# Split weights in 24 tiles of the first mixer, and one ScalarE pass a chunk behind six norms

## The reference

```
def hgrn2_mixer(h, w_in, lb, norm_g, w_out):
    proj = h @ w_in
    q, f_fw, f_bw, i_in, g = jnp.split(proj, 5, axis=-1)
    ...
    def gates(f_logit):
        f = lb + (1.0 - lb) * jax.nn.sigmoid(f_logit.astype(jnp.float32))
        return heads(jnp.log(f)), heads(1.0 - f)
    ...
    o = rms_norm(o_fw + o_bw, norm_g.reshape(HG_HEADS, HG_DV)) * jax.nn.silu(g)
    return o.reshape(B, S, D_MODEL) @ w_out
```

## Time and profile before

| | |
|---|---|
| median of three runs | 3061.45 us (3059.26 to 3065.03) |
| profiled execution | 3059.53 us, span 3057.8 us |
| instructions | 57758 |
| TensorE busy | 2936.9 us, 96% of the span |
| VectorE busy | 2234.3 us, 73% |
| ScalarE busy | 1633.3 us, 53% |
| granted TensorE clock, mean | 0.989 of full |
| bytes moved | 503.04 MB, 165 GB/s on average |

### The profile page before, as it was taken

One profiled execution on the slowest core, in us unless ns is written; L12 is line 12 of the kernel. 1 busy time (PEld: TensorE's weight loads), 2 busy tenths in 40 slices (PEclk: granted clock), 3 DMA queues, 4 the chain that ended last, 5 costly groups with the idle time before them and its releaser, 6 DMA issues.

```text
span 3057.8 us, 57758 instructions
## 1 busy us (share of the span) xinstructions
PE 2936.9 (96%) x19592; PEld 2665.4 (87%) x19592; DVE 2234.3 (73%) x4764; ACT 1633.3 (53%) x3372; POOL 62.1 (2%) x112
## 2 busy tenths in 40 slices
PE   7988999999999999999999999999999999998998
PEld 6888899999887778899999988888898889797896
DVE  6346498888779985649888877777585578656686
ACT  2113557778544443655777854444554267463574
POOL 3000000000001100000000000000000000000000
PEclk9999999999999999999999999999999999999999
DMA  9521454444478853445444455555441145432453
GB/s 397 200 76 55 146 187 161 152 164 139 159 258 309 308 200 118 144 155 186 158 153 163 139 172 187 190 186 190 136 138 63 56 164 177 144 132 79 145 174 117
DMA packets 137686, 503.04 MB, mean 165 GB/s; under 512 B 15312, under 2 KB 15440, under 8 KB 137264
## 3 DMA queue, kind: packets, MB, share of 16 engines
q1 hardware_dynamic: 122544, 445.63, 43.1%
q0 software_dynamic: 14976, 55.19, 5.0%
HBM read 498.65 MB, written 2.10 MB: 164 GB/s over the span
## 4 chain that ended last, share of the span: by engine, by line
PE 81%; DVE 5%; ACT 4%; issue 1%; DVEq 0%; ACTq 0%
PE PB L536 14%; PE PB L537 14%; PE PB L538 13%; PE PA L579 9%; PE PA L580 9%; PE PA L578 9%; PE PA L772 4%; PE PB L526 2%; DVE w_low L2223 2%; PE PA L984 1%; PE PA L1157 1%; PE PA L627 1%; ACT h_high L1301 1%; DVE BIG L2249 1%; ACT w_high L1198 1%
## 5 line engine op out<-in xcount | busy, mean ns | idle before, releaser
L1198 ACT ACTIVATE w_high<-ring 128x512 fp32r<-128x512 f32 x1548 | 962.3, 630 | 848.8 <-PE PA L580 466.4
L2223 DVE TENSOR_TENSOR w_low<-ring,w_high 128x512 fp32r<-128x512 f32 x1548 | 1050.7, 690 | 430.3 <-ACT w_high L1198 414.6
L536 PE MATMUL PB<-h_high,w_low 128*128 128x256 f32 x3792 | 1088.4, 287 | 30.4 <-DVE h_low L1889 20.7
L537 PE MATMUL PB<-h_low,w_high 128*128 128x256 f32 x3792 | 1071.8, 283 | 0.0
L538 PE MATMUL PB<-h_high,w_high 128*128 128x256 f32 x3792 | 1069.5, 282 | 0.0
L536 PEld LDWEIGHTS PB<-h_high,w_low 128*128 128x128 f32 x3792 | 725.2, 191 | 46.6 <-issue 25.0
L537 PEld LDWEIGHTS PB<-h_low,w_high 128*128 128x128 f32 x3792 | 719.4, 190 | 0.7 <-issue 0.5
L538 PEld LDWEIGHTS PB<-h_high,w_high 128*128 128x128 f32 x3792 | 718.4, 189 | 0.0
L578 PE MATMUL PA<-w_low,a_high 128*128 128x512 f32 x1200 | 470.3, 392 | 7.9 <-DVE a_low L2232 7.1
L579 PE MATMUL PA<-w_high,a_low 128*128 128x512 f32 x1200 | 476.3, 397 | 0.0
L580 PE MATMUL PA<-w_high,a_high 128*128 128x512 f32 x1200 | 474.0, 395 | 0.0
(11 more groups left out here) (334 smaller groups left out, 2587.3 us busy)
## 6 DMA issues: line engine op xcount, KB each, us to landing
ring<-tiles SPq DMA_DIRECT2D x842, 512.0 KB, 3.3
BIG<-ada POOLq DMA_DIRECT2D x96, 512.0 KB, 7.1
BIG<-skew POOLq DMA_DIRECT2D x4, 512.0 KB, 4.7
X<-x SPq DMA_DIRECT2D x1, 1024.0 KB, 5.8
skew<-BIG POOLq DMA_DIRECT2D x1, 1024.0 KB, 6.4
out<-X SPq DMA_DIRECT2D x4, 256.0 KB, 2.1
con<-consts SPq DMA_DIRECT2D x1, 911.0 KB, 8.8
BIG<-masks POOLq DMA_DIRECT2D x1, 768.0 KB, 8.4
```

What stands on the lines that cost most here:

```text
L536: mm(dst, lhs_l, high, start=start, stop=False, skip_group_check=True)
L537: mm(dst, lhs_h, low, start=False, stop=False, skip_group_check=True)
L1198: fn(tile_half(w_high, s, b), ring[:, at:at + HALF], ACT.Identity).then_inc(sem("high_ready"), 1)
L2223: tt(tile_half(w_low, s, b), ring[:, at:at + HALF], tile_half(w_high, s, b).bitcast(F32), ALU.subtract).then_inc(sem("low_ready"), 1)
```

## The change

The 40 tiles of `hg_in` become two runs: `hg_decays`, 16 whole tiles, and `hg_rest`, 24 split tiles. The activations of that mixer now lie in `HB`, since `w_high` lies over `H`, and are split as well: ScalarE rounds four pairs behind its eight affine passes, VectorE subtracts. The masks of the lower triangle move from the buffer of `w_low` into `TMP`. TensorE's sum over the partitions of vectors 2 to 5 stands behind 11 split tiles; the last of these vectors is accumulated by VectorE block by block between the splits of the first eight tiles, and the decays are made chunk by chunk between the others.

Behind the six norms ScalarE makes one pass a chunk, in place. The rounding of pairs 0 and 1 goes to VectorE (`HIGH_BY_ACT`), as a copy ahead of its subtraction; that of pairs 2 and 3 is one ScalarE pass each over both chunks, behind the in-place passes. Pair 0 is copied and subtracted ahead of VectorE's fourth scaling.

```diff
-    ("hg_in", 5 * DC), ("hg_out", DC), ("wq0", 2 * PEER_HEADS), ("keys0", 2), ("experts0", 2 * NKEYS),
+    ("hg_decays", 2 * DC), ("hg_rest", 3 * DC), ("hg_out", DC), ("wq0", 2 * PEER_HEADS), ("keys0", 2), ("experts0", 2 * NKEYS),
 ...
-        way_masks, w_low = overlaid("way_masks", 2 * TILE, ("w_low", 2 * TILE))
+        w_low = sb("w_low", 2 * TILE, F32R)
 ...
-        LOW_MASKS = way_masks[:, 0:PAIR_LEVELS * P]
+        LOW_MASKS = TMP[:, 0:PAIR_LEVELS * P]
 
         SUMS = ["experts0", "experts1", "down0", "down1"]
+        HIGH_BY_ACT = 2
 ...
-            def split_linear(name, order=(0, 1, 2, 3)):
+            def split_linear(name, order=(0, 1, 2, 3), first=0, last=None):
 
                 s0, (q0, n) = SPLIT_AT[name][0], product_at[name]
-                h0 = fresh_pairs(order)
+                h0 = None if first else fresh_pairs(order)
 
                 def body(k, it):
                     pe.wait_ge(taken, it * 4 + (q0 + k - 3))
                     split_product(product_slot(q0 + k), s0 + k, it, 4, h0 if k == 0 else None)
 
-                spans(pe, body, (0, n))
+                spans(pe, body, (first, n if last is None else last))
 ...
             pe.wait_ge(sem("mod_ready"), w.up(sem("mod_ready"), 2))
-            linear("hg_in", H, sem("h_ready"), 0, 3 * DC)
+            linear("hg_decays", HB, sem("h_ready"))
+            split_linear("hg_rest", last=11)
             ada(2, LATER)
-            linear("hg_in", H, None, 3 * DC)
-            all_taken("hg_in")
+            split_linear("hg_rest", first=11)
+            all_taken("hg_rest")
             pe.wait_ge(sem("mod_ready"), w.up(sem("mod_ready")))
 ...
-            def split_evacuate(run, first):
+            def split_evacuate(run, first, at=0, func=lambda j: ACT.Identity, edge=None):
 ...
+                edges = (2, first + 2, first + 3) if first else (2, 3)
 ...
-                    fn(BIG[:, bass.ds(it * (4 * T) + j * T, T)], product_slot(q0 + j),
-                       ACT.Identity).then_inc(taken, 1)
+                    fn(BIG[:, bass.ds(it * (4 * T) + (at + j * T), T)], product_slot(q0 + j),
+                       func(j)).then_inc(taken, 1)
 ...
-                spans(act, tile, (2, first + 2, first + 3, n) if first else (2, 3, n))
+                spans(act, tile, edges + ((edge + 2, n) if edge else (n,)))
                 copied(n - 2)
                 copied(n - 1)
 ...
@@ -1297,11 +1300,13 @@
                         act.wait_ge(sem("scaled"), w.up(sem("scaled")))
                     dk, g = dst[:, m * T:(m + 1) * T], gain[:, m:m + 1]
                     add = {} if shift is None else {"bias": shift[:, m:m + 1]}
-                    if split:
-                        fn(h_high[:, m * T:(m + 1) * T], dk, ACT.Identity, scale=g, **add)
                     ins = fn(dk, dk, ACT.Identity, scale=g, **add)
                     if m % 2:
                         ins.then_inc(sem(name), 1)
+                        w.up(sem(name))
+                        if split and m // 2 >= HIGH_BY_ACT:
+                            act.wait_ge(sem(name), w.value(sem(name)))
+                            fn(two(h_high, m // 2), two(dst, m // 2), ACT.Identity).then_inc(sem("pair_high"), 1)
 
             def norm_affine(i, split=True):
                 affine(X, p("ln_g", i * DC, DC), p("ln_b", i * DC, DC), "x_out", split)
@@ -1310,6 +1315,11 @@
 
                 if sub:
                     affine(HB, gains(layer, sub), modulation(layer, sub, 0), "whole_ready", split=True)
+                elif layer == 0:
+                    affine(HB, gains(layer, sub), modulation(layer, sub, 0), "h_ready")
+                    for i in range(DC // 2):
+                        act.wait_ge(sem("h_ready"), i + 1)
+                        fn(two(h_high, i), two(HB, i), ACT.Identity).then_inc(sem("pair_high"), 1)
                 else:
                     affine(H, gains(layer, sub), modulation(layer, sub, 0), "h_ready")
 ...
             modulated(0, 0)
-            evacuate("hg_in", big(0, 16 * T), ACT.Sigmoid, 0, 2 * DC)
-            evacuate("hg_in", big(16 * T, 16 * T), ACT.Identity, 2 * DC, 4 * DC)
-            evacuate("hg_in", HG_G, ACT.Silu, 4 * DC, 5 * DC)
+            for k in range(2):
+                evacuate("hg_decays", big(14 * k * T, 16 * T), ACT.Sigmoid, 14 * k, 14 + k)
+                split_high("hg_rest", k)
+            evacuate("hg_decays", big(15 * T, T), ACT.Sigmoid, 15)
+            split_evacuate("hg_rest", 0, 16 * T, lambda j: ACT.Identity if j < 2 * DC else ACT.Silu, 2 * DC)
             act.wait_ge(sem("ada_psum"), 2)
             split_high("hg_out", 0)
             split_high("hg_out", 1)
 ...
-            def scale(dst):
+            def scale(dst, name=None):
 
                 dve.wait_ge(sem("root_ready"), w.up(sem("root_ready")))
                 v.reciprocal(inv[:, :], inv[:, :]).then_inc(sem("dve_step"), 1)
                 dve.wait_ge(sem("dve_step"), w.up(sem("dve_step")))
                 for i in range(DC // 2):
+                    if i == DC // 2 - 1 and name is not None:
+                        split_fresh(dst, name, 0)
                     tt(chunks(two(dst, i)), chunks(two(X, i)), over(inv[:, :], 2), ALU.mult)\
                         .then_inc(sem("scaled"), 1)
+                if name is not None:
+                    for i in range(1, DC // 2):
+                        split_fresh(dst, name, i)
 ...
-            def split_whole(src, name):
-                for i in range(DC // 2):
-                    split_pair(src, name, i)
-
-            def split_x():
-                split_whole(X, "x_out")
-
-            def rms(name, dst, run=None):
+            def split_fresh(src, name, i):
+
+                dve.wait_ge(sem(name), w.up(sem(name)))
+                if i < HIGH_BY_ACT:
+                    v.tensor_copy(two(h_high, i), two(src, i)).then_inc(sem("dve_step"), 1)
+                    dve.wait_ge(sem("dve_step"), w.up(sem("dve_step")))
+                else:
+                    dve.wait_ge(sem("pair_high"), w.up(sem("pair_high")))
+                tt(two(h_low, i), two(src, i), two(h_high, i).bitcast(F32), ALU.subtract)\
+                    .then_inc(sem("h_split"), 1)
+
+            def rms(name, dst, run=None, split=None):
                 if name is not None:
                     dve.wait_ge(*added(name, DC - 1))
                 if run is not None:
                     split_low(run, 0)
                 w.up(sem("squares_ready"), DC // 2)
-                scale(dst)
+                scale(dst, split)
                 if run is not None:
-                    split_whole(dst, "whole_ready")
                     split_low(run, 1)
 ...
-                scale(X)
-                if run is not None:
-                    split_x()
+                scale(X, "x_out" if run is not None else None)
 ...
-            rms(None, H)
+            rms(None, HB)
             for k in range(DIRECT, DC):
                 ada_tile(1, k, 0, first=DIRECT)
             modulate(0, 1, PB, P)
             modulate(1, 2, PB[:, 1024:], P)
-            ada(2, LATER)
-            modulate(2, LATER)
-            for d, way in enumerate(HG["ways"]):
-                dve.wait_ge(taken, (d + 1) * DC)
-                for m in range(DC):
-                    s_ = slice(m * T, (m + 1) * T)
-                    ts(way["f"][:, s_], way["f"][:, s_], om[:, m:m + 1], lb[:, m:m + 1],
+            for i in range(DC // 2):
+                split_pair(HB, "pair_high", i)
+            ada(2, LATER - 1)
+            for k in range(3 * DC):
+                split_low("hg_rest", k)
+                if k < DC:
+                    ada_tile(LATER - 1, k, 0)
+                if k == 12:
+                    modulate(2, LATER)
+                d, m = divmod(k - DC, DC)
+                if d >= 0:
+                    f, s_ = HG["ways"][d]["f"], slice(m * T, (m + 1) * T)
+                    dve.wait_ge(taken, d * DC + m + 1)
+                    ts(f[:, s_], f[:, s_], om[:, m:m + 1], lb[:, m:m + 1],
                        ALU.mult, ALU.add).then_inc(sem("dve_step"), 1)
-                dve.wait_ge(sem("dve_step"), w.up(sem("dve_step"), DC))
+                    w.up(sem("dve_step"))
+            for way in HG["ways"]:
+                dve.wait_ge(sem("dve_step"), w.value(sem("dve_step")))
                 ts(way["k"], way["f"], -1.0, 1.0, ALU.mult, ALU.add).then_inc(sem("dve_step"), 1)
                 w.up(sem("dve_step"))
             dve.wait_ge(sem("dve_step"), w.value(sem("dve_step")))
@@ -2582,11 +2609,11 @@
             dve.wait_ge(sem("way_masks_loaded"), w.up(sem("way_masks_loaded"), 16))
             dve.wait_ge(taken, 3 * DC)
             decay_attention(HG, "hg_out")
-            all_taken("hg_in")
+            all_taken("hg_rest")
             gated_heads(HG_MIX, HG_HEADS, lambda h: p("hg_norm_g", h, 1), HG_G)
             scale_heads(HG_MIX, HG_HEADS)
             add_product("hg_out", modulation(0, 0, 2))
-            rms("hg_out", HB, "wq0")
```

(12 more changed lines are left out.)

2 lines of the change are left out of this document (1 added, 1 removed).

## The result

The changed kernel took 3029.03 us (median of four runs, 3025.99 to 3029.45), the kernel before 3060.36 us beside it (3058.54 to 3065.03): ratio 0.9894, 95% interval 0.9882 to 0.9907, so 1.1% faster. The forecast was 3032.6, with a range of 3024.5 to 3042. The profiled execution took 3028.78 us, its span is 3027.1, 30.7 shorter than before.

The account below looks back on a forecast made before the run. TensorE was taken as the bound, with 81% of the chain. 14.9 us from 24 split tiles plus 13.9 us from six norms made 28.8, giving 3032.6 us against the median of 3061.45; range 3024.5 to 3042.

Parts of the forecast that it names:

- 24 x 0.62 = 14.9: First mixer: each of 24 tiles, once split, falls from 3.45 to 2.83 us, gaining 14.9 us.
- Late transfers at no cost: First mixer: VectorE's later start delays transfers; tiles 16 to 19 still in time, cost 0, range 0 to 5; rival 0.10.
- room for two split tiles: First mixer: each tile may be split while two earlier ones are multiplied, so a late one has about a tile's time.
- my own signs of being wrong: TensorE waiting for w_low between 97 and 125, a modulation block after 115, extra table loads after tile 32, copies above 0.69.
- Keys' work at no cost: End of first mixer: VectorE's keys and queries finish before the mask selection could begin, margin 0.6 us, cost 0, range 0 to 2.
- VectorE's queue: First mixer: VectorE needs 2.71 of 2.83 us for the first eight split tiles, cost 0 to 2; slower rival 0.03.
- Tables: First mixer's unrolled tail: one ScalarE table load, in idle time; rival, a load at each change, 11 us less gain, 0.05.
- 2.56 us at a norm, 1.1 at `even_in`: Last pair's subtraction ends earlier behind six norms: 2.56 us gained at five, about 1.1 at the sixth.
- The clock as 0: TensorE's half-clock stretches behind the norms: up to 6.0 us more gain or 4.6 less, taken as 0.
- 28.8: Whole kernel: total forecast gain in us, 14.9 from the first mixer plus 13.9 from the six norms.
- clock up: Rival: none of the six norms pays half clock; total gain 34.8 us, 3027 us; chance 0.12.
- B: The norms' part, one ScalarE pass a chunk: 12.8 us at five norms plus 1.1 at the sixth, 13.9.

Follow-up runs that it names:

- e1: The changed kernel with only the first mixer's part (24 split tiles), the norms as before: 3047.0 us, ratio 0.9957 to the kernel before.
- e9: The changed kernel with eight more tiles split (32 split, 8 whole) and modulation blocks one per split tile: 3020.0 us, ratio 0.9877 to the kernel before.
- e6: The changed kernel with VectorE taking modulation group 2 ahead of the four subtractions of the first mixer's input: 3026.7 us, ratio 0.9882.
- e4: The changed kernel with all four pairs rounded by ScalarE (HIGH_BY_ACT = 0): 3033.9 us, ratio 0.9910 to the kernel before.
- e3: The changed kernel with all four pairs rounded by VectorE (HIGH_BY_ACT = 4): 3028.9 us, ratio 0.9895 to the kernel before.
- e2: The changed kernel with only the six norms' part, the first mixer as before: 3042.2 us, ratio 0.9937 to the kernel before.
- e11: The changed kernel with 32 tiles split and four filler products at the start (e9 plus that filler): 3017.6 us, ratio 0.9863.
- e7: The changed kernel with six filler products instead of five at the six norms: 3027.1 us, ratio 0.9885 to the kernel before.
- e8: The changed kernel with small filler products ahead of pairs 1 and 3 behind the six norms: 3029.1 us, ratio 0.9897 to the kernel before.
- e12: e11 with the small fillers between pairs of e8 added: 3019.0 us, ratio 0.9865 to the kernel before.

## Why the prediction was right

- *24 x 0.62 = 14.9.* Measured 14.92 between the same two takes, 14.95 in e1, and 5.03 for eight more tiles in e9. The pitches of before were all that it needed.
- *Late transfers at no cost.* Right in the sum, wrong in the order, and in part luck. I had tile 16 landed by 94 and tile 18 split by 102. Tile 16 was there at 95.8, and ScalarE waited for the next three as well. What covered it is what I had named for VectorE, room for two split tiles, and it was nearly used up: the first low half of tile 19 was done at 106.62, and TensorE took it up 0.05 us later. Between the same takes the changed kernel needs 123.36 us and the eight others with 24 split tiles 123.33 or 123.34, so the cost was at most some hundredths. One of my own signs of being wrong did come: the last modulation block was used at 116.74, not by 115. It cost nothing, as the sums were complete at 118.2 and TensorE wanted them behind its 11th split tile, at about 129. e6 removes most of the lateness and gains nothing in the median. In the changed kernel, the halves of tile 19, TensorE's load of the first of them, and the last block:

```profile
105.93 1.29 DVE L2241 TENSOR_TENSOR w_low<-ring,w_high 128x512 fp32r<-128x512 f32 x2 [0.81 <-ACT w_high L1200]
...
106.67 0.19 PEld L537 LDWEIGHTS PB<-h_high,w_low 128*128 128x128 f32 x1
...
116.74 1.28 DVE L1860 SCALAR_TENSOR_TENSOR BIG<-BIG,coef 128x1024 f32<-128x1024 f32 x1
```

- *Keys' work at no cost.* Margin 0.6 forecast, 0.73 measured.
- *VectorE's queue.* A block and two halves took it 2.40 us a tile once the tiles were there, from the fourth to the eighth (105.93, 108.33, 110.73), forecast 2.71.
- *Tables.* One load for the Silu, at 154.36 us, in idle time, and no other behind tile 32.
- *2.56 us at a norm, 1.1 at `even_in`.* The last pair stands at 6.89 or 6.90 at all five norms and at 6.15 at the sixth (forecast 6.86 and 6.12). TensorE's pauses at `up0` were forecast as 1.1, 1.0 and 0.9 us and are 1.26, 0.62 and 0.54. Only one stretch is without half clock before and after, from the scaling of `up0` to that of `odd_in`: 212.27 before, 209.7 to 210.5 in the eleven kernels with the new norms but e4, 2.2 less on the mean rather than 2.56. TensorE starts the second tile 7.76 us behind the scaling in ten of the eleven (7.67 in e3) and 10.30 before: the 2.54 are there. e2, e9 and e11 carry 2.5 to 2.6 of them to the next scaling. The others lose 0.1 to 0.7 on the way: six of them have 11 tiles that are 2.94 to 3.11 us apart late in `up0`, where the kernel before has 9; what sets the pace there no run shows. e4 starts the second tile at 9.08, 1.22 earlier than before, and keeps 0.33 of it. From `even_in` to `up0`, at the same 10.2 us of half clock, e1 stands at 299.89 and six kernels with the new norms at 298.2 to 298.4: 1.6, forecast 1.1. From `wq1` to `even_in`, all at 6.8 us, the old norms stand at 858.2 and 859.3 (before, e1), four kernels with the new ones at 856.5: 1.7 and 2.8, forecast 2.56.
- *The clock as 0.* The term that was mis-sized, in both parts: 3 us against the change ahead of the first of the six norms (14.9 became 11.95), 5 for it behind (13.9 became 18.8). That the two nearly cancel, so that 28.8 stands beside 30.7, is luck. The whole kernel before had 68 us at 0.50, the changed one 56. For the rest of the kernel the table gives the price. All kernels with the new norms but e4 lie within 1 us of one line: from 24 us at 0.50 and 2716.8 us to 37 and 2722.1, which is 0.39 us for each. Carried on to the 51 and 58 us of the old norms (beyond the measured points), the line leaves 10 to 13 us to the norms' own steps, and 6 to 9 to the clock. That is an estimate and no more: the two kernels with the old norms, before and e1, differ by 7 us of half clock and by 0.1 us of time. The 18.8 lies between my forecast and the rival "clock up", which had B at 19.9 and a chance of 0.12. Behind the norms ahead of `wq0`, `wq1`, `even_in`, `odd_in` and `up1`, the stretches were 6.8, 6.8, 3.4, 6.8 and 6.8 us before; now 3.4, 3.4, none, 3.4 and none. But e1, with the old norms, has 3.4, 3.4, none, 3.4 and 6.8, and 6.8 behind `up0`, where the kernel before had none. e4, whose pairs are later by 1.3 us, has 6.8, none, 3.4, none and 6.8. A shorter pause goes with fewer of them, in these profiles; that it causes this is argued, not shown, and e1 speaks against a part of it. e7, e8, e9 and e12 have none, and the fillers of e7, e8 and e12 don't show in the median, since stretches elsewhere come and go from profile to profile.

## What to carry to other kernels

Measure a change of pace between the same two events at either end of the loop, not by the kernel's time: there it came out to 0.1 us, while the two parts of the time were 3 and 5 us off the forecast, the first by the granted clock, the second in part by it. Late transfers and a full queue matter only when TensorE's own idle time shows them; here neither did, and so the step could go on from 24 tiles to 32, with the loads spread over the tiles. But compare when each half is ready with when it is used: at the tightest tile only hundredths of a microsecond were left, and a forecast of no cost that holds by so little is luck. And look for the pause that has TensorE-bound work right behind it: a filler there brought the products 1.5 to 2.7 us forward, while fillers behind six norms gave nothing that can be measured.

## What the runs showed of the hardware

A stretch of 3.4 us at 0.50 costs very different amounts. Where dense products follow it costs the most: from `even_in` to `up0` the length is 295.0 to 295.3 with 3.4 us at half clock, 296.6 with 6.8, 298.2 with 10.2 and 300.8 with 17.1, 1.4 us for each stretch on average and 1.6 for the first two. Half of 3.4 is 1.7. The Trainium skill, "TensorE: Matmul & The Clock Gate", section "HAM oscillation — how this bites in real kernels", works out the penalty of throttled time as one half of it; these rows come close, but only where TensorE sets the pace. Between the last take of the first mixer and the scaling of `wq0`, a stretch 16 us behind the take cost nothing (123.1 to 123.45 us with and without it), one at 262 to 270 us 1.4, and between the scalings of `wq0` and `experts0` it is 861.2 to 861.3 us without any and 862.0 to 862.8 with one, 0.7 to 1.6.

The same work doesn't always lose its clock. The stretch at 269.9 us in the changed kernel, shown with e1, lies behind 3.4 us in which TensorE was busy for 1.56; e9 has the same work with the same 1.56 ahead of it and keeps its clock:

```profile
262.40:265.80 3.40, 1.56 (x12) 1.22 (x11) 3.06 (x5) 1.29 (x3) 0.00 (x0) 1.00 0.00 0
265.80:269.20 3.40, 3.40 (x31) 3.40 (x31) 1.51 (x3) 1.28 (x3) 0.00 (x0) 1.00 0.03 7
```

So one trace of each kernel doesn't tell what a change does to the clock: the same program had 56 us at 0.50 in its first profile and 45 in its second.

The rounding copy of 128x512 on VectorE took 0.42 to 0.43 us, against 0.69 for a two-operand pass over the same and 0.287 for half as many columns.
